# RWKV stage: the newer tile's step is issued ahead of the older tile's in each round

## The chip, the cores and the metric

The kernel runs on one core of a Trainium2 chip. The metric is the device time of one execution in microseconds (us). The kernel before takes 2481.12 us (median of 3 runs, 2478.01 to 2484.82). All data are float32.

## The reference

The reference is two blocks on a sequence of 1024 tokens with 1024 features. The first block projects the input and mixes it in three ways: attention in a window of 128 tokens, a gated linear recurrence (RG-LRU), and an RWKV-7 recurrence. It then projects back and normalizes. The second block adds 16 tokens and runs two layers (a pooling mixer, then latent attention), each with a mixture of experts (32 experts of width 256, two for each token).

The change touches the RWKV-7 part alone. For each of 4 heads of 64 channels, it computes, token by token:

```
sa    = state @ (-kk_t)
state = state * w_t + sa (x) b_t + v_t (x) k_t
y_t   = state @ r_t
```

Then each head of y is normalized, a bonus term is added, and the result is gated.

## The kernel before

The kernel is one program with one written-out instruction list for each engine: TensorE (PE), VectorE (DVE), ScalarE (ACT), GpSimd (POOL) and SyncE. Each engine runs its own list strictly in order, and waits on semaphores for the others. The stages follow each other: projections and attention, preparation of the RWKV inputs (`pe_prep` and its siblings), the RWKV stage, the output projection (`pe_out1`), and the second block. `pe_out1` and its siblings begin with a wait for everything in the RWKV stage.

The RWKV stage works on 8 tiles of 128 tokens. A tile is two chunks of 64 tokens, and inside a chunk the recurrence is turned into products of 64x64 matrices. Each tile passes through 20 steps, numbered s. Steps 0 to 9 are the front: they need nothing of the state. Steps 10 to 19 are the back: they carry the state through the two chunks and finish the output.

The steps, by TensorE's part (`pe_rwkv`, line 982), and what drains each from PSUM (`act_rwkv`, line 1152; `dve_rwkv`, line 1206):

- s=0: `ab` (decay-weighted products, masked by DVE in lines 1221 and 1227) and eight transposes `tok` (line 1036, copied by ACT).
- s=1: `p2` (squares of the masked matrices; half copied by ACT in line 1161, half by DVE in line 1239). DVE also adds the identity (line 1252).
- s=2: `kr` (masked by DVE, line 1227).
- s=3: `p4` and `x1`. s=4: `p8` and `x2`. s=5: `akv` and `x3`. DVE adds or subtracts each x result (`combine`, line 1234); ACT copies `p8` and `akv`.
- s=6: `xt`, s=7: `q32` (both copied by ACT). s=8: `pb` (DVE, line 1234, two of 64x512). s=9: `q64` (ACT).
- s=10: `x64` (DVE, line 1234). It needs `q64` of the same tile. s=11: `gt` and `u0` (ACT).
- s=12 and 14: `sv`, the state product of a chunk (DVE, line 1286). s=13 and 15: `dv` and `ys`; DVE makes the new state of `dv` (lines 1297 and 1305), ACT copies `ys`.
- s=16: `yc` (DVE, line 1312). s=17: `mean` (DVE line 1317, then ACT squares in line 1198). s=18: `var` (ACT takes the root, line 1201).
- s=19: DVE alone: reciprocal (line 1323) and product (line 1325). GpSimd then applies weight and bonus (lines 872, 874 and 876), behind the product of each tile.

Two tiles are in the pipeline at a time. The generator `rounds()` (line 802) gives the order of (tile, step) pairs. PE, ACT and DVE all run their steps in that order (lines 984, 1154 and 1211); GpSimd doesn't use it. A round holds one front step of tile i and the back step of tile i-1 that is ten steps further.

The front steps use PSUM banks 0 to 3 as a ring (`fr`), the back steps banks 4 to 7 (`bk_`). A product may be written once the product four places before it in its own ring is drained. With 28 front products in a tile, `ab` takes the banks of `pb`, and the transposes take those of `q64` of the tile before. Each of the two data sets in SBUF (`sets[i % 2]`) belongs to every second tile.

In the first ten rounds, where only tile 0 is in flight, ACT, DVE and PE also run the RG-LRU (`act_lru`, `dve_lru`, `pe_lru`). Tile 1's data set lies over its storage, so ACT and DVE start on tile 1 only when it is finished (lines 977 to 980 hold its last steps).

Each matmul of float32 operands appears in the trace as two records. A 64x64 product with 8 matmuls is 16 records.

Of the kernel before, what the change touches and what calls it, by code (L numbers as in the profile page):

```python
# [18 lines left out]
NT = T // P  # L19
# [151 lines left out]
def build(nc, io):  # L171
    ctx = ExitStack()
    with ctx:
# [628 lines left out]
        def rounds():  # L802

            for r in range(10 * (NT + 1)):
                i, s = divmod(r, 10)
                if i:
                    yield i - 1, 10 + s
                if i < NT:
                    yield i, s

        def of_head(q):
            return 2 * (q % 2) + q // 2
# [169 lines left out]
        def pe_rwkv(e):  # L982
            wait_all(e, after_prep)
            for i, s in rounds():
                own = sets[i % 2]
                tk, GT, AKV, U0, SA, Q, N = (own[n] for n in ("tok", "GT", "akv", "u0", "SA", "Q", "N"))
# [165 lines left out]
        def act_rwkv(e):  # L1152
            wait_all(e, after_prep)
            for i, s in rounds():
                own = sets[i % 2]
                tk, GT, AKV, U0, Q = (own[n] for n in ("tok", "GT", "akv", "u0", "Q"))
# [49 lines left out]
        def dve_rwkv(e):  # L1206
            wait_all(e, after_prep)
            e.memset(STt[:, 0], 0.0).then_inc(*states.up())
            e.memset(sets[0]["STE"], 0.0).then_inc(*V.up())
            e.wait_ge(*masks_in.at(2))  # L1210
            for i, s in rounds():
                own = sets[i % 2]
                GT, U0, SA, N, X1, X2 = (own[n] for n in ("GT", "u0", "SA", "N", "X1", "X2"))
# [1772 lines left out]
```

## Time and profile before

| | |
|---|---|
| Median of 3 runs | 2481.12 us |
| The profiled execution: its own time | 2481.37 us |
| Its span | 2479.6 us |
| PE busy | 2155.0 us, 87% of the span |
| DVE busy | 845.3 us, 34% |
| ACT busy | 591.3 us, 24% |
| RWKV stage on PE | from 452.95 to about 690 us |
| Mean granted TensorE clock | 0.923 |

Busy shares are means over all stages. The RWKV stage is a small part of the span with much shorter instructions than the rest, so it has to be read by itself. In a timeline row the first number is the start, the second the time from the start of the merged group to its end, and the bracket gives the idle time before it and what ended that.

### The profile page before, as it was taken

The numbers are of one execution on the slowest core, as the hardware profiler recorded it, in microseconds if no ns is written. First come the engines' busy times: TensorE is split into PE (matmuls) and PEld (weight loads), VectorE is DVE, ScalarE is ACT, GpSimd is POOL, SyncE is SP. The second block draws the span as 40 slices with busy tenths as digits, with TensorE's granted clock in tenths as the row PEclk, the third lists the DMA queues.
The fourth block names the chain that finished last, engine by engine and source line by source line (L and its number), as shares of the span: only waits on it lengthen the run. The fifth ranks groups of instructions, "written<-read, shape, count | busy, mean of one in ns | idle before, by whom it ended". The sixth has DMA issues, their size and how long they took to land. (4 is left out here: it accounts for less than half of the span.)

```text
span 2479.6 us, 27540 instructions
## 1 busy us (share of the span) xinstructions
PE 2155.0 (87%) x10876; PEld 1246.0 (50%) x10876; DVE 845.3 (34%) x1865; ACT 591.3 (24%) x1404; POOL 211.5 (9%) x305
## 2 busy tenths in 40 slices
PE   8999986468789784999996899999999949999990
PEld 4545542267634663444442565677674424444440
DVE  0115444466605434212112453344351141121115
ACT  1013323153301220111112343333331111111112
POOL 0000001201125110000000100000000000000002
PEclk9999988688889896999998899999999969999995
DMA  3500000000021116999996300000010047999956
GB/s 119 204 22 35 18 1 0 3 2 3 3 103 51 56 51 246 347 367 372 361 375 238 123 3 1 1 1 1 1 69 28 34 179 291 366 375 363 370 232 222
DMA packets 46200, 349.30 MB, mean 141 GB/s; under 512 B 6256, under 2 KB 6576, under 8 KB 36208
## 3 DMA queue, kind: packets, MB, share of 16 engines
q1 hardware_dynamic: 32176, 296.97, 30.8%
q0 software_dynamic: 13888, 50.47, 5.9%
q8 instruction: 92, 1.51, 0.3%
q14 instruction: 44, 0.36, 0.0%
HBM read 292.82 MB, written 54.59 MB: 140 GB/s over the span
## 5 line engine op out<-in xcount | busy, mean ns | idle before, releaser
L202 PE MATMUL psum<-arena 128*128 128x512 f32 (+7 forms) x9328 | 1990.3, 393 | 204.1 <-DVE arena L1901 25.9
L202 PEld LDWEIGHTS psum<-arena 128*128 128x128 f32 (+3 forms) x9328 | 1068.2, 176 | 1057.4 <-issue 879.6
L2032 DVE TENSOR_TENSOR arena<-psum,arena 128x256 f32<-128x256 f32 x64 | 27.2, 425 | 540.2 <-ACT arena L2076 540.2
L2110 POOL DMA_INDIRECT arena<-xn_rows,arena x64 | 60.2, 941 | 820.3 <-PE psum L1999 588.2
L2076 ACT ACTIVATE arena<-psum 128x256 f32<-128x256 f32 x64 | 24.7, 386 | 408.3 <-PE psum L202 408.3
L1455 ACT ACTIVATE arena<-arena 128x1024 f32<-128x1024 f32 x43 | 45.4, 1056 | 259.5 <-DVE arena L2744 101.6
L2657 ACT ACTIVATE arena<-psum,arena 128x1024 f32<-128x1024 f32 (+8 forms) x72 | 50.3, 700 | 188.5 <-DVE arena L2693 188.5
L1161 ACT ACTIVATE arena<-psum 64x256 f32<-64x256 f32 (+4 forms) x176 | 67.1, 389 | 115.4 <-PE psum L202 82.2
L2069 ACT ACTIVATE arena<-psum 128x512 f32<-128x512 f32 x64 | 38.3, 598 | 185.5 <-PE psum L202 185.5
L1999 PE MATMUL psum<-arena 128*128 128x128 f32 x512 | 68.2, 277 | 10.8 <-DMA arena<-xn_rows,arena 10.8
L1999 PEld LDWEIGHTS psum<-arena 128*128 128x128 f32 x512 | 59.2, 144 | 12.2 <-DMA arena<-xn_rows,arena 11.1
L2097 DVE COPY arena<-psum 128x512 f32<-128x512 f32 x64 | 44.3, 692 | 61.1 <-PE psum L202 61.1
L2057 ACT ACTIVATE arena<-psum 128x512 f32<-128x512 f32 x64 | 38.3, 598 | 94.1 <-PE psum L1999 94.1
L2686 DVE TENSOR_TENSOR psum<-psum,arena 128x128 f32<-128x128 f32 (+2 forms) x72 | 20.3, 283 | 103.5 <-PE psum L202 103.2
L2218 DVE SCALAR_TENSOR_TENSOR arena<-arena 128x1024 f32<-128x1024 f32 (+1 forms) x34 | 43.5, 1281 | 28.6 <-DMA arena<-expert_rows,arena 27.1
L2688 DVE TENSOR_REDUCE arena<-psum 128x1 f32<-128x1024 f32 (+8 forms) x72 | 50.8, 706 | 2.5
L1234 DVE TENSOR_TENSOR arena<-arena,psum 64x256 f32<-64x256 f32 (+1 forms) x80 | 37.8, 472 | 35.6 <-PE psum L202 34.0
L2612 PE MATMUL psum<-arena 128*128 128x128 f32 x352 | 48.9, 273 | 0.0
L2709 DVE COPY arena<-psum 128x512 f32<-128x512 f32 (+3 forms) x48 | 22.8, 490 | 76.0 <-PE psum L2612 75.9
L373 DVE TENSOR_TENSOR arena<-psum,arena 128x512 f32<-128x512 f32 x16 | 11.1, 691 | 109.8 <-ACT arena L354 109.8
L2090 DVE COPY arena<-psum 128x512 f32<-128x512 f32 x64 | 43.6, 681 | 12.6 <-PE psum L1999 12.6
L359 ACT ACTIVATE arena<-psum 128x512 f32<-128x512 f32 (+1 forms) x26 | 15.5, 597 | 134.5 <-PE psum L202 134.5
(290 smaller groups left out, 1336.1 us busy)
## 6 DMA issues: line engine op xcount, KB each, us to landing
arena<-in_w_exp SPq DMA_DIRECT2D x64, 3072.0 KB, 11.7
expert_rows<-arena SPq DMA_DIRECT2D x80, 512.0 KB, 3.8
arena<-in_x SPq DMA_DIRECT2D x16, 512.0 KB, 5.2
xn_rows<-arena SPq DMA_DIRECT2D x16, 512.0 KB, 2.6
arena<-in_w_out SPq DMA_DIRECT2D x8, 512.0 KB, 7.3
arena<-in_w_o SPq DMA_DIRECT2D x1, 4096.0 KB, 13.2
out<-arena SPq DMA_DIRECT2D x8, 512.0 KB, 2.7
arena<-in_rows SPq DMA_DIRECT2D x6, 512.0 KB, 6.6
```

The costliest lines, as they stand in the source:

```text
L202: return e.matmul(out, lhsT, rhs, start=start, stop=stop, skip_group_check=True)
L1161: e.activation(dst, src, ACT.Copy, bias=0.0).then_inc(*ring.drain((i, name), "S"))
L1455: return e.activation(junk, h[:, s, :], ACT.Square, accum_out=sq_sum[:, s:s + 1])
L1999: m = e.transpose(four(ring.bank[key])[:, k, :], xe[:, P * (4 * hf + k):P * (4 * hf + k + 1)], ident)
L2057: e.activation(y.xt[b % 2][:, 4:8, :], four(y.ex.bank[key]), ACT.Copy, bias=0.0).then_inc(*y.ex.drain(key, "S"))
L2090: e.tensor_copy(y.xt[b % 2][:, 0:4, :], four(y.ex.bank[key])).then_inc(*y.ex.drain(key, "V"))
L2097: e.tensor_copy(y.y[b % 3][:, half_cols(0)], y.ex.bank[key]).then_inc(*y.ex.drain(key, "V"))
L2110: e.indirect_dma_start(out=xe, out_offset=None, in_=xn_dram[:, :], in_offset=bass.IndirectOffsetOnAxis(idx.bitcast(I32)[:, block:block + 1 ...
L2218: e.scalar_tensor_tensor(out=h[0:n, s, :], in0=c[j][0:n, :], scalar=gates[0:n, s, j:j + 1], in1=h[0:n, s, :], op0=ALU.mult, op1=ALU.add).t ...
L2612: m = e.transpose(four(sd.bank[key])[:, j, :], pb[:, kp:kp + P], ident)
L2657: e.activation(pb[0:n, p0:p1], part_bank(key).bank[key][0:n, 0:p1 - p0], ACT.Exp, bias=mx[0:n, 0:1], scale=SCALE, accum_out=rsu[0:n, u:u + ...
L2688: e.tensor_reduce(mx[0:n, u:u + 1], bk[0:n, 0:p1 - p0], AX.X, ALU.max).then_inc(*V.up())
```

## The change

In `rounds()` the two `yield` statements are swapped. In each round every engine takes the front step of tile i first and the back step of tile i-1 behind it.

```diff
             for r in range(10 * (NT + 1)):
                 i, s = divmod(r, 10)
+                if i < NT:
+                    yield i, s
                 if i:
                     yield i - 1, 10 + s
-                if i < NT:
-                    yield i, s
```

No instruction is added or removed, and the order inside each PSUM ring stays. Nothing changes in the first ten rounds (no older tile) and the last ten (no newer tile).

## Rows read from the trace of the kernel before

**Rows 1.** Windows: stretch, length, busy PE PEld DVE ACT POOL, granted clock, DMA share, GB/s.

```profile
514.74:674.24 159.50, 128.35 (x3249) 116.20 (x3249) 105.99 (x254) 64.89 (x168) 13.52 (x24) 0.89 0.01 3
```

**Rows 2.** Timeline of PE, one cycle of the pipeline and the last tile's x64.

```profile
607.42 1.84 PE L202 MATMUL psum<-arena 64*64 64x64 f32 x48 [0.88 <-ACT arena L1161]
609.19 1.97 PE L1036 MATMUL psum<-arena 128*128 128x128 f32 x8
611.09 2.77 PE L202 MATMUL psum<-arena 64*64 64x64 f32 x120
614.37 2.63 PE L202 MATMUL psum<-arena 64*64 64x64 f32 x80 [0.50 <-DVE arena L1286]
617.21 0.68 PE L202 MATMUL psum<-arena 64*64 64x64 f32 x16 [0.21 <-DVE arena L1239]
618.11 3.43 PE L202 MATMUL psum<-arena 64*64 64x64 f32 x104 [0.22 <-DVE arena L1234]
621.87 1.32 PE L202 MATMUL psum<-arena 64*64 64x64 f32 x20 [0.33 <-DVE arena L1234]
623.43 2.73 PE L202 MATMUL psum<-arena 64*64 64x64 f32 x52 [0.24 <-ACT arena L1161]
627.76 0.87 PE L202 MATMUL psum<-arena 64*64 64x64 f32 x16 [1.60 <-DVE arena L1234]
629.48 1.97 PE L202 MATMUL psum<-arena 64*64 64x64 f32 x48 [0.84 <-ACT arena L1161]
...
674.24 0.68 PE L202 MATMUL psum<-arena 64*64 64x64 f32 x16 [0.88 <-ACT arena L1161]
```

**Rows 3.** Windows, columns as in rows 1: stretches around changes of the clock.

```profile
604.30:607.50 3.20, 0.76 (x18) 0.68 (x20) 3.08 (x3) 0.76 (x2) 0.00 (x0) 1.00 0.02 5
607.70:610.90 3.20, 3.20 (x54) 2.94 (x50) 2.62 (x8) 0.55 (x1) 2.25 (x4) 0.50 0.00 0
...
515.50:518.80 3.30, 3.11 (x48) 2.59 (x44) 3.23 (x3) 0.15 (x1) 0.00 (x0) 0.50 0.00 0
...
669.10:672.40 3.30, 1.82 (x36) 1.52 (x36) 1.20 (x2) 1.17 (x3) 0.00 (x0) 1.00 0.02 5
672.50:675.80 3.30, 1.36 (x32) 1.15 (x32) 3.00 (x5) 0.76 (x2) 0.88 (x2) 1.00 0.00 0
...
624.70:628.00 3.30, 1.56 (x42) 1.31 (x42) 1.68 (x3) 0.69 (x2) 0.00 (x0) 1.00 0.00 0
...
559.90:563.20 3.30, 2.45 (x53) 2.24 (x51) 2.57 (x5) 0.76 (x2) 1.56 (x3) 0.50 0.02 5
```

**Rows 4.** Timeline of DVE, ACT and POOL from pb's drain on.

```profile
626.26 1.40 DVE L1234 TENSOR_TENSOR arena<-arena,psum 64x512 f32<-64x512 f32 x2 [2.60 <-PE psum L202]
627.69 1.75 DVE L1323 RECIPROCAL arena<-arena 128x256 f32<-128x256 f32 x1
628.60 0.78 ACT L1161 ACTIVATE arena<-psum 64x256 f32<-64x256 f32 x2 [3.19 <-PE psum L202]
629.48 0.43 DVE L1325 TENSOR_TENSOR arena<-arena 128x256 f32<-128x256 f32 x1
630.01 0.88 POOL L872 TENSOR_SCALAR arena<-arena 128x128 f32<-128x128 f32 x2 [19.49 <-DVE arena L1325]
```

**Rows 5.** Timeline of DVE, the four mask products of ab, first and last.

```profile
609.39 0.29 DVE L1221 TENSOR_TENSOR arena<-psum,arena 128x128 f32<-128x128 f32 x1
...
610.26 0.55 DVE L1227 TENSOR_TENSOR arena<-psum,arena 128x384 f32<-128x384 f32 x1
```

**Rows 6.** Groups by line and shape, 539.9 to 654.1: count, busy us, mean ns, idle before.

```profile
L1234 DVE TENSOR_TENSOR arena<-arena,psum 64x256 f32<-64x256 f32 x41 | 17.2, 419 | 7.5 <-PE psum L202 6.7
```

**Rows 7.** Timeline of PE in the second block: the same transposes at full clock.

```profile
845.14 1.07 PE L1783 MATMUL psum<-arena 128*128 128x128 f32 x8
```

**Rows 8.** Timeline of PE and DVE where tile 1 enters.

```profile
512.74 1.12 PE L202 MATMUL psum<-arena 64*64 64x64 f32 x16 [1.60 <-DVE arena L1234]
...
517.39 1.23 DVE L980 TENSOR_TENSOR arena<-arena 128x1024 f32<-128x1024 f32 x1
```

## The prediction

> **What bounds the kernel now.** I read the page's busy shares first: TensorE (PE) is busy 87% of the span, which says nothing about a stage of 160 us with 33 ns matmuls. So I went to the stretches of the RWKV stage. From the first tile's x64 to the last tile's (514.74 to 674.24) seven pipeline cycles take 159.5 us, 22.8 us each; PE is busy 128.4 us of them, DVE 106.0, ACT 64.9, and PE's mean granted clock is 0.89 [rows 1]. All three alternate in a ring of short handshakes, so next comes PE's timeline of one cycle [rows 2]. The reader is to see where PE stands idle: 0.50 (DVE's sv drain), 0.21, 0.22, 0.33, 0.24, 1.60 (before q64, for DVE's pb) and 0.84 us (before x64, for ACT's copy of q64), 3.94 us in a cycle that runs from 607.42 to 629.48, 22.06 us. The last two stand beside each other, because x64 of a tile is issued right behind its q64.
>
> The third view is the clock. At 604.3 to 607.5 PE is busy 0.76 of 3.2 us; right behind it the clock is at its lower level, 1.2 GHz of 2.4, from 607.7 to 610.9, with PE busy all the time [rows 3]. So the pair of gaps is paid twice. A mean of 0.89 over 159.5 us is 22% of it, 35 us, at half clock. Had PE only worked in these, it would have lost 17.5 us; they begin in the wait before x64, so I take 15 to 17.
>
> **The change part by part.** Nothing is added or removed; only what lies between two dependent steps moves. On PE the steps alternate front, back, front, back as before. The partners change: what a back step had before it now stands behind it. SyncE and GpSimd don't follow this order; GpSimd's work on a tile still starts behind DVE's product of step 19.
>
> I walk one new cycle at full clock. Durations from start to start: sixteen records take 0.52 (80 records take 2.63, so 0.033 each), and 0.16 more until their modelled end. The eight transposes take 0.95 at full clock (1.07 with the end [rows 7], 1.97 at half [rows 2]). ab and kr have four matmuls side by side, so I take 0.45 and 0.70; mean and var 0.70 each. A reader starts 0.1 after PE's modelled end; PE follows a reader by 0.10 to 0.12 (628.60 + 0.78 to 629.48) [rows 2, 4]. A pair of x results takes DVE 0.87 (2 x 0.42 and a start) [rows 6].
>
> The gaps of the new cycle:
> - Before q64: pb's drain still costs 1.60 behind pb, but var (0.70) now lies in between instead of ahead: 0.90.
> - Before the transposes: they take q64's banks, so they wait for ACT's copy, 0.18 + 0.78 + 0.10 = 1.06 behind q64, which ab covers for 0.45 and whose first half lets the first four go: 0.2. The old 0.84 before x64 is gone, since ab and the transposes now lie under it.
> - Before p2: this is what is late next. DVE does, in its order, pb 1.40, the reciprocal 1.75, the product 0.43, and only then the new tile's masks, 609.39 to 610.81, 1.42 [rows 4, 5]. With the handshakes and 0.07 between them p2 can start 5.27 behind pb's end. PE reaches it after 1.60 + q64 0.52 + ab 0.45 + 0.2 + transposes 0.95 + x64 0.52 = 4.24: gap 1.03. Before, gt and u0 also stood ahead of p2, and the x64 drain stood ahead of the masks.
> - Before dv: the sv drain now stands behind kr's masks on DVE, but p4 and x1 (1.56) cover both: 0; x1 itself waits 0.08 for kr's banks. The old 0.50 is gone.
> - Before x2: DVE runs the sv drain, p4's copy and x1 in a row: 0.27. Before x3: x2's drain with only sv and akv (0.72) as cover: 0.47, where 0 was. Before xt: x3's drain 1.17 against dv and ys 0.77: 0.40.
> - Before mean: yc's drain, 0.79, against q32 0.52: 0.25. Before pb and var: 0.1 and 0.1.
>
> Sum: 0.90 + 0.20 + 1.03 + 0.08 + 0.27 + 0.47 + 0.40 + 0.25 + 0.2 = 3.8 us. That is hardly less than the old 3.94: the reordering by itself moves the gaps rather than removing them. PE's work of a cycle is 22.06 - 3.94 = 18.1, less the 1.7 that the half clock of 607.7 to 610.9 costs: 16.4. A new cycle at full clock is then 20.2 us; the old one at full clock would have been 20.3.
>
> So the gain depends on the clock. The old pair 1.60 and 0.84, with 0.9 of work in between, becomes 0.90 and 1.03 with 2.6 of work in between; in the idlest stretch as long as those of rows 3, PE is busy 1.9 us. The rows show both outcomes: PE was busy 0.76 of 3.2 us (604.3 to 607.5) and 1.56 of 3.3 (624.7 to 628.0) before it fell, and 1.82 of 3.3 (669.1 to 672.4) where it stayed full after (672.5 to 675.8) [rows 3]. The new cycle is nearest to the last. I take full clock in cycles 2 to 7.
>
> The entry of tile 1 is special. DVE is in the RG-LRU until 518.62 [rows 8], so the masks run 518.65 to 520.1 and p2 starts at 520.2, as if the cycle had begun at 517.0 (p2 stands 3.2 behind its cycle's start). And the clock: it is at half until 518.8 with PE busy 3.11 of 3.30; the new PE is done with x64 by 517.8 and idle until 520.2. With 2.45 busy of 3.3 it stayed at half elsewhere [rows 3]. I charge the first cycle 5 us at half clock, 2.5 us (bounds 0 and 3.4).
>
> The last tile's x64 starts 1.06 behind the last q64: 517.0 + 7 x 20.2 + 2.5 + 1.06 = 662.0, where it was 674.24 [rows 2]: 12.2 us earlier. Everything behind it (the last tile's back steps, and the stages that wait for the whole of this one) moves with it unchanged. The profiled execution took 2481.37 us around a span of 2479.6, as good as the median 2481.12. 2481.4 - 12.2 = 2469.2 us. Bounds of the cycle: 19.6 (the parts summed one by one give this) to 20.7 (every new gap 0.05 larger), so 2465 to 2473, and 2462.5 if the first cycle loses nothing.
>
> One rule bears on the masks. GpSimd's work on a tile starts 0.1 behind DVE's product [rows 4], and in the new order the masks start at that very moment. In 607.7 to 610.9 GpSimd is busy 2.25 of 3.2 us [rows 3], and the masks from 609.39 on still take 0.29 and 0.55 [rows 5]. The Trainium skill, "SBUF — State Buffer", section "SBUF: two separate sides", says that VectorE and GpSimd share an exclusive port, and that a VectorE operation takes part in it only with two SBUF inputs or in a 2-port mode; the masks have one input in PSUM, so by the rule too they go free. The identity's addition (line 1252) has two SBUF inputs and now comes as GpSimd's last operation ends; by the rule it could wait for that operation, and the sum would be up to about 4 us more. No run here shows the two beside each other.
>
> **The rivals.**
> - The clock falls as often as before. For it: the new gaps are still two in one cycle, and a stretch with 1.56 busy came before a fall [rows 3]. Against it: behind 1.82 busy it stayed. Half stretches over q64, ab, transposes and x64 meet the 1.03 us slack before p2, so of 17.5 us some 7 are swallowed: 12.2 + 2.5 - 10.3 = 4.4 saved, 2477 us.
> - Nothing comes of it: PE, DVE and ACT still alternate the same steps, the gaps are as long (3.8 for 3.9), and the clock's losses fall where PE is the bound: 12.2 + 2.5 - 17.5 = -2.8, 2484 us. Against it: the wait before x64, which deepens the idle stretch, is certainly covered.
> - Slower: DVE's in-order queue. Reciprocal and product (2.2 us) of the old tile stand directly ahead of the masks, and p2 starts a run of PE work without slack (p2, gt, u0, kr: some 2.9 us). If the clock falls just there and stays low for twice the stretch, as at 559.9 with 2.45 busy [rows 3], each cycle loses 3.4 us and is 23.6 instead of 22.8: with the start's shift 9 us more, 2490 us. It turns the sign from a loss of 2.1 us in each cycle on (4.2 us at half clock). Against it: DVE's chain is the same length, and PE has more work beside it than before.
> - The gaps shrink further than I find (p2's wait disappears, as the reciprocal gets under earlier PE time): 19.2 a cycle, 2460 us.
>
> **How the numbers follow.** My forecast gets 0.60, the clock as before 0.19, nothing 0.08, slower 0.08, the large gain 0.05. The likeliest is 2469 us. The range 2461 to 2482 takes in the forecast, the clock rival and half of the rest. A difference of 0.3%, 7.4 us, is about what a measurement can tell from no change here. Faster by more: 0.57 of the forecast, 0.05 of the large gain, 0.03 of the clock rival, 0.65. Within: 0.03 + 0.16 + 0.07 = 0.26. Slower: 0.09.
>
> **What would show it.** In the new trace: no wait before x64 for ACT, and x64 behind the transposes; a wait of about 1.0 before p2 for line 1227, one of 0.9 before q64, new ones of 0.3 to 0.5 before x3 and xt; DVE's reciprocal, product and masks with nothing between them; a cycle of 20.2 us and a mean clock of 0.96 or more from 540 on. If cycles are 20.2 at a clock of 0.87, my gap sum is wrong; if they are over 21.5 with the gaps as listed, the clock is. Wholly wrong would be a cycle of 23 or more.

## The result, and the profile after

The changed kernel takes 2463.15 us (median of 4 runs, 2459.46 to 2464.55), the kernel before 2479.57 us beside it. The ratio on record is 0.9921, with a 95% interval of 0.9907 to 0.9936: 16 to 23 us less, where 12 were forecast. (The quotient of the two medians is 0.9934, inside that interval.) A second set gave 0.9923 (0.9911 to 0.9935). The range was 2461 to 2482 us: the median lies in it, and 0.9921 of 2479.57 us, 2460.0 us, just under its low end. The sign and most of the waits came out as forecast. The gain is larger, and it doesn't come from the clock alone: about half of it is the order itself, which the prediction put at 0.1 us a cycle.

The profiled pair differs by 17.5 us in span (2479.6 to 2462.1), and 17.1 us of it lie in the RWKV stage. From the first product of tile 0 to the first load of w_out the stage takes 243.1 us before (452.95 to 696.04) and 226.0 us after (453.12 to 679.13). I read all experiments by this length too, since the rest of the kernel varies from one profile to the next, over all ten between 2233.5 and 2240.4 us, which is as much as some of the effects.

PE's timeline of the changed kernel, one cycle and the last tile's x64. The rows that answer are [rows 2].

```profile
621.11 7.51 PE L202 MATMUL psum<-arena 64*64 64x64 f32 x248 [0.84 <-DVE arena L1227]
628.94 1.49 PE L202 MATMUL psum<-arena 64*64 64x64 f32 x40 [0.32 <-DVE arena L1234]
630.70 2.89 PE L202 MATMUL psum<-arena 64*64 64x64 f32 x68 [0.26 <-DVE arena L1234]
633.82 1.79 PE L202 MATMUL psum<-arena 64*64 64x64 f32 x36 [0.24 <-ACT arena L1161]
636.58 1.15 PE L202 MATMUL psum<-arena 64*64 64x64 f32 x48 [0.96 <-DVE arena L1234]
637.69 1.09 PE L1036 MATMUL psum<-arena 128*128 128x128 f32 x8
638.71 0.68 PE L202 MATMUL psum<-arena 64*64 64x64 f32 x16
640.31 7.51 PE L202 MATMUL psum<-arena 64*64 64x64 f32 x248 [0.92 <-DVE arena L1227]
...
657.33 0.68 PE L202 MATMUL psum<-arena 64*64 64x64 f32 x16 [0.88 <-ACT arena L1161]
```

The reader is to see four things. The cycle is 19.20 us (621.11 to 640.31). The x64 of 638.71 follows the transposes with no wait. The transposes take 1.09 us where they took 1.97. And the waits are those foretold by name, in sum 2.70 us: p2 for line 1227 (0.92 in the usual case), x3 for line 1234 0.32, xt 0.26, pb 0.24, q64 0.96.

DVE's timeline of the same kernel around them, to be held against [rows 4, 5]:

```profile
635.07 1.40 DVE L1234 TENSOR_TENSOR arena<-arena,psum 64x512 f32<-64x512 f32 x2 [1.02 <-PE psum L202]
...
636.51 1.75 DVE L1323 RECIPROCAL arena<-arena 128x256 f32<-128x256 f32 x1
...
638.29 0.42 DVE L1325 TENSOR_TENSOR arena<-arena 128x256 f32<-128x256 f32 x1
...
638.75 0.29 DVE L1221 TENSOR_TENSOR arena<-psum,arena 128x128 f32<-128x128 f32 x1
...
639.62 0.55 DVE L1227 TENSOR_TENSOR arena<-psum,arena 128x384 f32<-128x384 f32 x1
```

pb, reciprocal, product and masks stand in one unbroken row of 5.1 us, from 635.07 to 640.17; p2 starts at 640.31.

Windows of the changed kernel (columns as in [rows 1]): the seven cycles, from the transposes of tile 1 to the last x64, and five single cycles, from p2 to p2.

```profile
514.82:657.33 142.51, 117.73 (x3219) 106.95 (x3217) 105.78 (x254) 63.08 (x168) 13.45 (x24) 0.96 0.01 3
520.39:541.75 21.36, 18.50 (x464) 17.12 (x465) 14.53 (x37) 9.12 (x24) 1.40 (x3) 0.87 0.01 3
541.75:560.95 19.20, 16.29 (x464) 14.80 (x465) 14.66 (x37) 9.00 (x24) 2.25 (x5) 1.00 0.01 3
560.95:582.25 21.30, 16.82 (x464) 15.08 (x465) 14.64 (x37) 8.99 (x24) 2.24 (x5) 1.00 0.02 3
582.25:601.85 19.60, 16.32 (x464) 14.76 (x465) 14.65 (x37) 9.00 (x24) 2.24 (x5) 1.00 0.01 3
601.85:621.11 19.26, 16.39 (x464) 14.95 (x465) 14.65 (x37) 8.99 (x24) 2.25 (x5) 1.00 0.02 4
```

From 541.75 on the clock is 1.00 throughout, where [rows 1] have 0.89. The first cycle is the exception that was foretold. The third is not: it is 2.1 us longer at full clock and with the same DVE work. Most of that is time in which PE stood idle for nothing that the profile shows, 1.16 us after the first 101 records of the long run, plus a longer wait before q64 (1.31):

```profile
560.95 2.46 PE L202 MATMUL psum<-arena 64*64 64x64 f32 x101 [0.92 <-DVE arena L1227]
564.57 5.30 PE L202 MATMUL psum<-arena 64*64 64x64 f32 x147 [1.16 <-issue]
...
578.51 1.15 PE L202 MATMUL psum<-arena 64*64 64x64 f32 x48 [1.31 <-DVE arena L1234]
```

### The profile page after: what moved, and what is told of

It is laid out like the page before. It is cut to its first block and busy times, and to the rows that moved or that the text cites. A ratio compares the mean times of both kernels' runs of the same rounds, so it can differ in the third digit from the quotient of the medians.

```text
span 2462.1 us, 27540 instructions
## 1 busy us (share of the span) xinstructions
PE 2144.9 (87%) x10876; PEld 1237.4 (50%) x10876; DVE 845.3 (34%) x1865; ACT 589.0 (24%) x1404; POOL 211.1 (9%) x305
## 5 line engine op out<-in xcount | busy, mean ns | idle before, releaser
L2069 ACT ACTIVATE arena<-psum 128x512 f32<-128x512 f32 x64 | 38.2, 597 | 185.5 <-PE psum L202 185.5
L1234 DVE TENSOR_TENSOR arena<-arena,psum 64x256 f32<-64x256 f32 (+1 forms) x80 | 37.8, 472 | 21.4 <-PE psum L202 19.9
```

## The experiments

All times beside runs of the kernel before on the same chip. "Stage" is the length defined above, from the profile. The last two columns are the mean of cycles 2 to 7, from the q64 of tile 1 to that of tile 7, and the granted clock in that stretch. Added lines shift the line numbers in the listings: by 7 in e1 (L1241 is line 1234, L1234 is line 1227), by 9 in e2, by 2 in e6.

| kernel | median us | ratio (95%) | stage us | cycles 2 to 7, mean us | clock in them |
|---|---|---|---|---|---|
| before | 2479.6 to 2481.5 | 1 | 243.1 | 22.6 | 0.89 |
| changed | 2463.15 | 0.9921 (0.9907-0.9936) | 226.0 | 19.6 | 1.00 |
| changed, again (e8) | 2463.21 | 0.9923 (0.9911-0.9935) | 225.6 | 19.5 | 1.00 |
| e1: before, waits filled | 2474.59 | 0.9976 (0.9965-0.9988) | 233.5 | 21.1 | 1.00 |
| e2: PE alone reordered | 2555.29 | 1.0299 (1.0282-1.0316) | 315.0 | 32.9 | 0.70 |
| e3: DVE, ACT alone | 2565.34 | 1.0339 (1.0324-1.0353) | 330.3 | 34.7 | 0.73 |
| e6: swap in round 0 only | 2480.01 | 0.9993 (0.9984-1.0002) | 243.0 | 22.1 | 0.94 |
| e4: changed, entry filled | 2464.50 | 0.9937 (0.9923-0.9951) | 225.2 | 19.6 | 1.00 |
| e5: changed, step 19 late | 2461.47 | 0.9928 (0.9914-0.9943) | 222.2 | 19.0 | 1.00 |
| e7: e4 and e5 together | 2459.59 | 0.9918 (0.9905-0.9930) | 219.9 | 18.9 | 1.00 |

**e1: how much is the clock?** In the old order, work that nothing reads is put into the two waits.

```diff
+                def filler(ring, key, n):
+                    wait_all(e, ring.free(key))
+                    for _ in range(n):
+                        mm(e, ring.bank[key][:, 0:P], ident, ident, True, True)
...
                 elif s == 9:
+                    filler(fr, (i, "q64_0"), 3)
                     by_chunk(fr, "q64", [(of(CT64), of(XB))], *both("pb"))
                 elif s == 10:
+                    filler(bk_, (i, "x64_0"), 1)
```

> The kernel before, in its old order, with idle time of TensorE filled: three 128x128 matmuls of the identity ahead of the wait before q64, one ahead of the wait before x64, each into the bank that the waiting product overwrites. Their results are never read, nothing is reordered. Theory (the clock carries a large part): the two gaps no longer drop the clock, so a cycle of the RWKV stage goes from 22.8 to 20.3-20.6 us and the seven cycles from 159.5 to 142-146 us, 2479.6 - 15 = 2465 us. Rival (the clock only follows, the order of the steps is what pays): the gaps stay as long, the cycle stays above 22 us, 2477 to 2482 us. Sub-question for both: if the cycle at full clock is 20.3 and the changed kernel's is 19.2, then the order alone is worth 1.1 us a cycle; if my gap sum was right it is worth 0.1.

PE's timeline of e1, one cycle, and below it two windows (columns as in [rows 1]), the seven cycles and this one:

```profile
539.47 1.15 PE L202 MATMUL psum<-arena 64*64 64x64 f32 x48 [0.46 <-ACT arena L1168]
540.55 1.09 PE L1041 MATMUL psum<-arena 128*128 128x128 f32 x8
541.58 0.94 PE L202 MATMUL psum<-arena 64*64 64x64 f32 x32
542.72 2.05 PE L202 MATMUL psum<-arena 64*64 64x64 f32 x88 [0.20 <-DVE arena L1234]
...
558.84 1.10 PE L202 MATMUL psum<-arena 64*64 64x64 f32 x18 [0.74 <-DVE arena L1241]
560.40 1.15 PE L202 MATMUL psum<-arena 64*64 64x64 f32 x48 [0.46 <-ACT arena L1168]
```

```profile
515.59:665.96 150.37, 126.66 (x3305) 113.06 (x3305) 105.98 (x254) 63.10 (x168) 13.51 (x24) 0.99 0.01 3
539.47:560.40 20.93, 17.93 (x473) 15.99 (x473) 14.68 (x37) 8.99 (x24) 2.25 (x4) 1.00 0.01 2
```

The clock rose to 1.00 in cycles 2 to 7, although TensorE's useful work and its order are the old ones. The seven cycles fell from 159.5 to 150.4 us, the stage by 9.6 of the 17.1 us. So the clock is a cause and not a companion, but it carries about half of the stage's gain, not nearly all. By time its share is smaller, 0.24% (0.12 to 0.35) of the 0.79%; in e1's profile the rest of the kernel takes 3.1 us longer than in the one before (2239.6 for 2236.5), and no run says why.

In the mean of cycles 2 to 7 the three kernels take 22.6, 21.1 and 19.6 us: 1.5 us a cycle for the clock and 1.5 for the order, the idle times of the changed kernel's third and fourth cycle included. In a cycle without a stall, the old order at full clock needs 20.9 us where I had 20.3, and the new one 19.2 where I had 20.2. Both theories as I had put them were wrong in size.

The rows also show why half clock costs less than its length. The blocks of 539.47 and 540.55 take 1.6 us less than those of 607.42 and 609.19 in [rows 2], but behind them a wait of 0.20 for the masks (line 1227) appears that was hidden before, and the cycle is 1.1 us shorter (20.93 for 22.06).

**e2 and e3: whose order is it?** `rounds_old` yields in the old order. In e2 ACT and DVE use it and PE the new one, in e3 the reverse.

```diff
-            for i, s in rounds():        # act_rwkv and dve_rwkv in e2, pe_rwkv in e3
+            for i, s in rounds_old():
```

> The new order on TensorE alone; VectorE and ScalarE keep the old one. Theory: PE's order gives the cover for q64's drain and so the clock; VectorE now takes x64's result ahead of the new masks, so p2 waits 0.87 us longer, and the other small drains come in the wrong order: cycle 19.2 + 0.9 to 1.5, stage 143 to 149 us instead of 142.5, 2468 to 2473 us, clock still full or nearly. Rival (VectorE's order is the part that pays): 2477 us or more.

> The mirror of e2: VectorE and ScalarE in the new order, TensorE in the old one. In e2 the readers asked for the older tile's product first while TensorE made it second, and the cycle went to 33.4 us, since each front product's drain waited behind the back step's. Theory: it is the mismatch that costs, not TensorE's order, so the mirror is slow too: the back step's product, made first, is drained only behind the front step's, and the state chain stretches: cycle 28 to 34 us, 2520 to 2560 us. Rival (the front chain alone is critical, and the readers now take it first): cycle 21 to 24 us, 2470 to 2490 us.

My theory for e2 failed by 80 us. e3 was forecast after e2, and its cycles (32.4 to 38.2 us) and time (2565 for 2520 to 2560) came out a little above the theory and far from the rival. The timeline of PE and DVE in e2 shows how, and below it the window of the cycle from 581.69 on:

```profile
593.07 1.46 PE L202 MATMUL psum<-arena 64*64 64x64 f32 x40 [0.30 <-DVE arena L1236]
594.51 0.47 DVE L1306 SCALAR_TENSOR_TENSOR arena<-psum,arena 128x64 f32<-128x64 f32 x2 [1.58 <-PE psum L202]
...
595.47 0.69 DVE L1248 COPY arena<-psum 64x512 f32<-64x512 f32 x1
...
596.31 0.68 PE L202 MATMUL psum<-arena 64*64 64x64 f32 x16 [1.78 <-DVE arena L1248]
...
597.21 1.94 PE L202 MATMUL psum<-arena 64*64 64x64 f32 x40 [0.22 <-DVE arena L1243]
```

```profile
581.69:613.22 31.53, 21.28 (x465) 19.54 (x465) 14.66 (x37) 9.22 (x24) 2.24 (x4) 0.76 0.01 2
```

p4 and x1 are ready first, but DVE's list asks for dv, which PE makes behind them. DVE copies p4 (L1248) only after dv (L1306) and its state, so PE waits 1.78 us with nothing left to do: in the matched order DVE drains p4 and x1 while PE makes dv and ys. A product made first and drained second has no such cover, whichever way the mismatch goes. The waits also bring the clock down: of the 12.3 us that this cycle is longer than one of the changed kernel (31.53 for 19.20), PE's busy time is 5.0 (21.28 for 16.29), and the rest is idle time. So in this cycle it is waits first and clock second. The small waits of DVE's order that I added up (0.9 to 1.5 us) are beside the point.

**e6: is it the tile boundary or the inner rounds?**

```diff
-                if i:
+                if s == 0 and i < NT:
+                    yield i, s
+                if i:
                     yield i - 1, 10 + s
-                if i < NT:
+                if s and i < NT:
                     yield i, s
```

> The old order, with the two steps swapped in the first round of each ten only (front step 0 ahead of x64), on all three engines. Theory: the wait before x64 goes, but gt then waits for x64's drain, which stands on VectorE behind reciprocal, product and masks: 5.27 + 0.87 behind pb's end, where TensorE arrives after 4.24, so a wait of 1.7 to 1.9 us instead of 0.84; the five small waits of the inner rounds stay at 1.5 us, the wait before q64 at 1.60. Cycle at full clock 21.9 to 22.2, the clock still drops: 22.5 to 23.5 us, 2476 to 2485 us. Rival (removing the pair of waits at the tile boundary is the whole gain): cycle under 21 us, 2468 us or less.

PE's timeline of e6, a cycle at full clock:

```profile
561.72 1.15 PE L202 MATMUL psum<-arena 64*64 64x64 f32 x48 [1.61 <-DVE arena L1236]
562.83 1.09 PE L1038 MATMUL psum<-arena 128*128 128x128 f32 x8
563.85 0.68 PE L202 MATMUL psum<-arena 64*64 64x64 f32 x16
566.19 2.80 PE L202 MATMUL psum<-arena 64*64 64x64 f32 x120 [1.65 <-DVE arena L1236]
569.49 2.63 PE L202 MATMUL psum<-arena 64*64 64x64 f32 x80 [0.50 <-DVE arena L1288]
```

As the theory had it: the wait for ACT before x64 is gone, one of 1.65 for x64's drain stands before gt, q64 still waits 1.61 and dv 0.50. The stage is 243.0 us, unchanged. But the boundary alone does not only rename its wait: cycles 2 to 7 take 22.1 us (22.5 to 23.5 were forecast) where the kernel before takes 22.6, as the clock stays up in some of them, but the first one, where tile 1 enters, takes 26.5 us from q64 to q64 where it took 24.3 and gives that back. The gain needs the inner rounds as well, where var and p2 come into the right places.

**e4: the first cycle.**

```diff
                 elif s == 1:
+                    if i == 1:
+                        filler(bk_, (0, "gt_0"), 5)
                     by_chunk(fr, "p2", ...
```

> The changed kernel with five 128x128 matmuls of the identity on TensorE in the wait before tile 1's p2 only, into a bank that is empty and is overwritten later. Theory: the first cycle (21.4 us, clock 0.87) ran some 4 us at half clock because PE was idle for 2.55 us while the clock was low; filled, it is 19.2 to 19.8 and the kernel 1.5 to 2.2 us faster than the changed one, 2461 us. Rival (the first cycle is long for VectorE's RG-LRU work, not for the clock): no change, 2463 us.

Window of e4, the first cycle:

```profile
521.26:540.62 19.36, 16.33 (x464) 14.87 (x465) 14.54 (x37) 8.99 (x24) 1.40 (x3) 1.00 0.02 4
```

It is 19.36 us at full clock where the changed kernel has 21.36 at 0.87, with the same DVE work, so its length was the clock. The stage gained only 0.8 us, since tile 0 reached its q64 1.2 us later in this build (61.0 us after the stage's start, not 59.8), which stays unexplained. The kernel's time can't be told from the changed one's, where 1.5 to 2.2 us less were forecast.

**e5: what sets p2's wait?** DVE's part of step 19 moves for tiles 0 to 5 (the normal place stays for the last two).

```diff
+                late = i - 2
+                if late >= 0 and s in (7, 8):
+                    e.wait_ge(*bk_.empty((late, "var")))
+                    half = own["dev"][:, s - 7, :]
+                    e.reciprocal(half, half).then_inc(*V.up())
+                if late >= 0 and s == (9 if i == NT - 1 else 11):
+                    y2 = yb[:, :, P * late:P * (late + 1)]
+                    e.wait_ge(*V.last())
+                    e.tensor_tensor(y2, y2, own["dev"], ALU.mult).then_inc(*y_norm.up())
...
-                elif s == 19:
+                elif s == 19 and i >= NT - 2:
```

> The changed kernel with step 19 of tiles 0 to 5 taken from between pb's drain and the new masks: VectorE does the reciprocal in two halves in the idle time of rounds 7 and 8 of a later tile (one after yc's sum, one after mean's subtraction) and the product in its round 1. Theory: p2's wait (0.92 us) is set by the chain pb 1.40, reciprocal 1.75, product 0.42, masks 1.42; without the middle two it falls to 0.1-0.3, the cycle from 19.2 to 18.4-18.6 and the kernel by 4 to 6 us to 2458 us. Rival (the halves push pb's drain or the masks of kr, and PE waits there instead): cycle 19.0 to 19.6, 2461 to 2466 us.

PE's timeline of e5, the end of one cycle and the long run of the next two:

```profile
536.56 1.15 PE L202 MATMUL psum<-arena 64*64 64x64 f32 x48 [0.96 <-DVE arena L1234]
537.67 1.09 PE L1036 MATMUL psum<-arena 128*128 128x128 f32 x8
538.69 8.39 PE L202 MATMUL psum<-arena 64*64 64x64 f32 x264
...
557.16 3.34 PE L202 MATMUL psum<-arena 64*64 64x64 f32 x117
561.22 5.30 PE L202 MATMUL psum<-arena 64*64 64x64 f32 x147 [0.72 <-issue]
```

x64 and p2 now run without a break (264 records), and the cycle is 18.47 us: the chain of reciprocal and product was what p2 waited for. pb's drain was not pushed (q64 waits 0.96 as before). In four of the seven cycles an idle time of 0.55 to 0.72 us for nothing that the profile shows took most of that back. The stage is 3.8 us shorter. By time nothing of it can be told: the ratio is 0.9928 where the changed kernel has 0.9921 and 0.9923, and in this profile the rest of the kernel takes 3.3 us longer (2239.4 for 2236.1).

**e7: both.**

> The changed kernel with both additions: step 19 late on VectorE, and the wait at tile 1's entry filled on TensorE. Theory: the two are independent, cycles of 18.5 us and a first one of 19.4: the stage is 220 to 222 us where the changed kernel's is 226, and the kernel 4 to 6 us faster than the changed one, 2458 us. Rival (with p2's wait gone TensorE has no slack left in the long run of products, so unexplained stalls of 0.6 us there, already seen with step 19 late, eat it): stage 223 us or more, 2461 us.

The stage is 219.9 us, 5.7 less than the changed kernel's beside it (225.6), as the theory had it. The time is 2459.6 against 2463.2 us; the intervals of the two ratios overlap almost wholly (0.9905 to 0.9930, 0.9911 to 0.9935), so a gain in time over the changed kernel is not shown.

## Why the prediction was right or wrong

- The sign, and that only the RWKV stage moves: right.
- x64's wait goes: right, it is 0. The masks behind reciprocal and product are late next: right in name and nearly in size, 0.92 for 1.03, and shown by e5. q64's wait: 0.96 for 0.90. Behind the last q64, where no new tile covers it, x64 still waits 0.88, as before.
- The inner gaps: those before x3 (0.32 for 0.47) and xt (0.26 for 0.40) are there. The one before pb is 0.24 for 0.1. The ones before x2, mean and the transposes (0.27, 0.25, 0.2), and the small ones before x1 and var, do not show as separate waits.
- Full clock in cycles 2 to 7: right, 1.00. The first cycle at half clock: right and shown by e4, 21.4 us for 22.7.
- The sum is the step that failed: "PE's work of a cycle is ... 16.4. A new cycle at full clock is then 20.2 us". I had counted the new gaps from the start of a block plus its issue time, and PE's work from the profile's idle times, which begin at the modelled end of the last matmul. Each stop has 0.16 us between the two (0.52 of issue against 0.68 in the profile). The old cycle, from which the 16.4 comes, has seven stops: 1.1 us counted twice, once as work and once as gap. The window of 541.75 to 560.95 shows on which side it was too much: PE's work is right (16.29 for 16.4), and its idle time is 2.9 us where the sum of gaps has 3.8. The same parts added with one convention had given 19.6 in my own working, which I named as a bound and did not believe. Measured: 19.2. That is 7 us over seven cycles.
- "That is hardly less than the old 3.94: the reordering by itself moves the gaps rather than removing them": wrong for the same reason. In the profile's own counting the gaps went from 3.94 to 2.70, and from seven stops to five. e1 against the changed kernel gives 1.5 us a cycle for the order in the mean, and 1.7 between cycles without a stall.
- The clock's share, "15 to 17" us: too large. e1 gave 9.1 over the seven cycles. I had charged the half clock for every microsecond of it, but a part of these was spent in waits that it does not lengthen, and a part of what full clock gave back went into waits it uncovered (the 0.20 in e1).
- The clock's share is no term of the sum that gives 662.0; the cycle is. That the time missed by 6 us and not by more is in part luck: the stalls of the third cycle (2.1 us), which no step had, go against the cycle's error. From 662.0 to the measured 657.33: the usual cycle 7 x -1.0, the first cycle another -0.3, the stalls of the third and fourth cycle +2.5, the later start of tile 0 +0.2, sum -4.6.
- Of the rivals, neither the clock nor DVE's queue took anything back. The one for a larger gain came nearest, with its cycle of 19.2 and its 2460 us, but for another reason than it names: p2's wait did not disappear. Its chance of 0.05 was too small by the same sum.

## What to carry to other kernels

When two chains share in-order engines, ask of each wait which step of the other chain stands in it, and give every engine the same order: here the same swap on TensorE alone cost 3.0%, on VectorE and ScalarE alone 3.4%. Look also for a step that ends one tile's chain and stands ahead of the one that starts the next tile's: moving it gave 0.7 us of a cycle of 19.2 in the profile of e5, though nothing that the time shows. Count work and gaps by one convention, starts to starts, before you compare sums that differ by a tenth.

## What the runs showed of the hardware

- In the kernel before, TensorE's clock fell to 1.2 GHz around the pair of waits before q64 and x64 (1.60 and 0.84 to 0.88 us). It stayed at 2.4 GHz in the changed kernel, with waits of 0.96 and 0.92 us and 2.8 us of matmuls between them. Reordering and filling with unused matmuls both kept it up. The length of the waits alone doesn't decide: in e6 the same 1.61 us before q64 left it at 2.4 GHz in one cycle and not in another, as two windows behind that wait show (columns as in [rows 1]):

```profile
561.70:566.20 4.50, 2.83 (x74) 2.47 (x74) 4.37 (x9) 1.84 (x4) 2.08 (x4) 1.00 0.01 4
...
628.00:633.00 5.00, 4.10 (x72) 3.51 (x68) 4.05 (x8) 1.95 (x4) 2.24 (x4) 0.66 0.02 5
```

- How much a half-clock stretch costs depends on what it meets: e1 gave 9 us in all here, where half of the 35 us would be 17.5.
- The masks take 0.29 and 0.55 us beside GpSimd's work ([rows 5]), and the same where GpSimd rests (at 519.55 and 519.76 of the kernel before). The identity's addition, with two SBUF inputs, takes 0.53 to 0.54 us in the changed kernel, where it begins 0.4 us into GpSimd's last operation, and 0.42 before, where nothing runs beside it:

```profile
L1252 DVE TENSOR_TENSOR arena<-arena x8: 421/532/539, 470.6 to 641.0; 128x256 f32<-128x256 f32 x8
```

That line of the changed kernel gives the shortest, median and longest duration in ns. The section of the Trainium skill that the prediction names ("SBUF — State Buffer", "SBUF: two separate sides") says that of two such operations the one that starts first holds the shared port for its whole length and the other is blocked. The masks agree with it. The addition agrees in kind, but not in size: waiting for the other's end (542.66, where it starts at 542.41) would have cost it 0.25 us, and it loses 0.11. The profile's spans on GpSimd are rough, so the 0.25 is an estimate. No wait of PE is put down to this addition, and the up to 4 us of the prediction did not come.
- PE stands idle in the long run of small matmuls for 0.15 to 1.41 us with no semaphore behind it. In e5 the place moves by 25 to 27 records from one cycle to the next (after 117, 142, 169 and 196 records), as a fixed length of the instruction list would that doesn't divide the cycle's. That points to the supply of instructions. The traces bear it out: in the ten profiles 20 such idle times fall into the seven cycles, and each ends 1.2 to 1.6 us behind the end of a transfer of 16 KB of the kind "instruction" on DMA queue q8, though these transfers lie 3.6 us or more apart. For the 1.16 us of the changed kernel the transfer ends at 563.33 and PE goes on at 564.57; for the 1.41 us of e4 it is 602.70 and 604.10. No run tested it, so the cause is not shown. From 538 to 656 us the changed kernel has 23 of them:

```profile
q8 instruction: 23, 0.38, 1.3%
```
